# One program block for the first block's stages from retention to routing, with waits in place of the barriers between them

## The chip, the cores and the metric

The kernel runs on one core of a Trainium2 chip. The metric is the device time of one execution in microseconds (us), the median over runs. TensorE (PE in the profile) multiplies matrices and writes into PSUM. VectorE (DVE) and ScalarE (ACT) work on tiles in SBUF and PSUM, GpSimd (POOL) works on SBUF, and SyncE (SP) mostly issues transfers. Each of the five has its own instruction queue, and they are kept in step by semaphores.

## The reference, cut to what matters

The program computes one pass through three different model blocks on 512 tokens of width 1024. The change touches only the first of them:

```python
h = modulate(rms_norm(x, g_mix), sh_a, sc_a)
u = h @ w_in
rq, rk, rv, rg, aq, ak, av, ga, gb = jnp.split(u, pts, axis=-1)
ret = retention(rq, rk, rv, rg)
att = dilated_attention(aq, ak, av, rel_bias)
merged = jax.nn.sigmoid(ga) * (ret @ w_ret_o) + jax.nn.sigmoid(gb) * (att @ w_att_o)
x = x + gt_a[:, None, :] * (merged @ w_o)
h = modulate(rms_norm(x, g_ffn), sh_f, sc_f)
x = x + gt_f[:, None, :] * moe(h, w_router, b_router, w1, b1, w2, b2)   # top 4 of 32 experts
```

`retention` has four heads. `dilated_attention` has four heads in each of three groups. `moe` begins with router scores, the choice of four experts per token and the lists of tokens by expert; after that come the experts' matrices.

## The kernel before

**The stages.** `block1` runs, in this order: the entry with the first modulation sections (`enter`); `retention`; `sigmoid_gate` for the first gate (stage `gate_a`); `linear_split` for the retention's output matrix (`ret_o`); `dilated` (stage `att`, with the later modulation sections between its heads); `sigmoid_gate` for the second gate (`gate_b`); `attention_out` (`att_o`, L2792 on); `add_residual` (`w_o`, with the second norm); `route`; `mixture` (the experts).
**Weights.** They stream through `ring`, six slots of one chunk each. SP issues the transfer of chunk n + 6 when chunk n has been used (`refill`, L171; semaphore `chunk_used`). Most products are full-precision results made of two rounded parts: a chunk has two halves ("places"), ACT rounds a half into `split_w` (L318, the high part), POOL subtracts to get the low part (L323), and PE then does 24 products for the half (high by high, low by high, high by low; L523, L397, L720). Place 0 of `split_w` becomes free when PE has used place 0 of the chunk before (`first_used`), place 1 when it has used the whole chunk before (`chunk_used`). `SplitAhead` lets a stage make place 0 of the next stage's first chunk at its end. `Forward` goes further at the end of retention: both halves of the first chunk of `gate_a` are made and multiplied there, around the transposes of the last head's output (L1454).

**Order of work on an engine.** It is the order in which the functions are written. In a `linear_split` stage ACT rounds the two halves for unit j and then takes the results of unit j - 1 out of PSUM (`take`); only the last unit's result is taken with nothing behind it but the barrier. In `route` ACT first rounds two halves of the experts' first chunk (`act_first_high`, L2213) and then copies the router's partial sums (L2067). DVE does small preparations, then `dve_low` (L2219), then the logits (L2100) and the whole choice. PE begins with eight products of the router's weights with `hT` (L2020). `hT` is written just ahead of it by `Norm.act_evac` (L959, four tiles of it by ACT) and `Norm.dve_evac` (L996, the other four by DVE).

Of the kernel before, what the change touches and what calls it, by code (L numbers as in the profile page):

```python
# [28 lines left out]
KD = D // P  # L29
# [52 lines left out]
class Kit:  # L82

    def __init__(self, nc, ctx, A, out, stream):
        self.nc, self.ctx, self.A, self.out, self.stream, self.scoped = nc, ctx, A, out, stream, []
        self.ring = self.sb(ctx, "ring", [P, RING, SLOT])
# [20 lines left out]
        self.x_source, self.x_loaded = A["x"][0].rearrange("(t p) d -> p t d", p=P), self.sem("x_loaded")  # L108

# [90 lines left out]
def linear(K, stage, kind, src, per_unit, act=None, dve=None, act_runs_ahead=2):  # L200
# [19 lines left out]
    with nc.Block() as block:  # L220
# [323 lines left out]
def linear_split(K, stage, kind, src, per_unit, act=None, dve=None, act_runs_ahead=2, paired=True, tiles=None,  # L544
                 after=None, guests=(), lead=None, parts=None, hold=False, loads=None, onward=None,
                 source=None, aside=None, asked=False):
# [16 lines left out]
    with ExitStack() as ctx:  # L563
# [22 lines left out]
        def split_source(eng, i):  # L586
# [79 lines left out]
        def tensor(pe):  # L666
# [108 lines left out]
        if not hold:  # L775
            with nc.Block() as block:
# [342 lines left out]
def enter(K, C, M, norm, onward):  # L1119
# [6 lines left out]
    with nc.Block() as block:  # L1126
# [180 lines left out]
def enter_turned(K, dst, pair, asked):  # L1307

    with ExitStack() as ctx:  # L1310
        N = Norm(K, "b2_norm", ctx, K.mods3[:, 0, :], None, dst, pair, K.x)
        onward = Onward(K, "b2_qkv", "N", pair, N)
        with K.nc.Block() as block:
# [24 lines left out]
def add_residual(K, stage, src, per_unit, gate=None, norm=None, final=None, guests=(), lead=None, parts=None, loads=None,  # L1338
                 onward=None, source=None, asked=False):
# [7 lines left out]
    def dve(j, banks, wait_tile):  # L1347
        for t in range(NT):
# [9 lines left out]
            if norm and j:  # L1358
# [3 lines left out]
                 guests=guests, lead=lead, parts=parts, loads=loads, onward=onward, source=source, asked=asked)  # L1362
# [47 lines left out]
def retention(K, pair, retpair, spare, name, rel, hot, jobs):  # L1410
# [9 lines left out]
    with ExitStack() as ctx:  # L1420
# [16 lines left out]
        with nc.Block() as block:  # L1437
# [159 lines left out]

def sigmoid_gate(K, stage, pair, dst):

    linear_split(K, stage, "T", pair, 1,
           act=lambda j, banks: K.nc.scalar.activation(dst[:, 2 * j:2 * j + 2, :], banks, ACT.Sigmoid))
# [105 lines left out]
def dilated(K, pair, attT, T0, T12, M):  # L1708
# [11 lines left out]
    with ExitStack() as ctx:  # L1720
# [10 lines left out]
        with nc.Block() as block:  # L1731
# [6 lines left out]
            def _(pe):  # L1738
# [16 lines left out]
                for h in range(AH):  # L1755
# [3 lines left out]
                    for g in range(AG):  # L1759
                        W.tiles(pe, n + g, pair, ps[:, 2 * g:2 * g + 2, :])  # L1760
                        if h and g == 0:
                            M.pe_total(pe, 2 * h - 1)
                    if h:
                        pe.wait_ge(copied, 4 * h)
                        pe.wait_ge(M.evac, 2 * h)
                    W.tiles(pe, n + 3, pair, ps[:, 6:8, :])
# [102 lines left out]
            def _(ve):  # L1869
# [15 lines left out]
                M.dve_spread(ve)  # L1885
                for h in range(AH):
# [18 lines left out]
                M.dve_mods(ve, 1)  # L1905

# [64 lines left out]
def route(K, R, mix):  # L1971
# [4 lines left out]
    A = K.A  # L1976
# [11 lines left out]
    with ExitStack() as ctx:  # L1988
# [18 lines left out]
        with nc.Block() as block:  # L2007
# [9 lines left out]
            def _(pe):  # L2017
                pe.wait_ge(K.loads, K.loads_n)
                for k in range(KD):
# [2688 lines left out]
```

## Time and profile before

| what | us |
|---|---|
| median of 3 runs | 3601.08 |
| lowest and highest run | 3599.22, 3602.8 |
| span of the profiled execution, first to last instruction | 3591.9 |
| what lies around the span, against the median | 9.2 |
| PE busy in the span | 3383.5 |
| DVE, ACT, POOL busy | 2046.8, 1772.5, 1050.0 |
| from the end of `enter` to the start of the experts, about | 690 (94 to 783) |

The page of the profile gives busy time by engine, the span in 40 slices, the queues and the costliest groups. The trace behind it can be asked for a timeline of a stretch (which merges equal instructions of an engine), for busy time and granted clock in given windows, and for what one line waited for.

### The profile page before, as it was taken

How to read it: one execution, taken by the hardware profiler on the slowest of the kernel's cores; microseconds unless marked ns; L12 is line 12 of the kernel's file. 1: busy time of each engine (PE TensorE's matmuls, PEld its weight loads, DVE VectorE, ACT ScalarE, POOL GpSimd, SP SyncE). 2: the span in 40 equal slices, each digit the busy share in tenths (PEclk: the TensorE clock that was granted, in tenths of full speed). 3: DMA queues.
4: the chain of work that ended last, by engine and by line, in shares of the span. 5: the costliest groups of instructions: out<-in, count | busy, mean ns of one | idle time of the engine just before them, and what ended most of it. 6: DMA issues, size and time to landing. Idle time of an engine off the chain costs nothing. (4 is left out here: it accounts for less than half of the span.)

```text
span 3591.9 us, 55463 instructions
## 1 busy us (share of the span) xinstructions
PE 3383.5 (94%) x20916; PEld 2733.5 (76%) x20916; DVE 2046.8 (57%) x2356; ACT 1772.5 (49%) x2340; POOL 1050.0 (29%) x432
## 2 busy tenths in 40 slices
PE   7999999979999999999999898899999987799997
PEld 4877777668888888888888683678887766678876
DVE  3320122179999999999999725411153155346665
ACT  3222333258888878788887624332243343133333
POOL 1324222212323232323232140144443310034443
PEclk9999999989999999999999999999999988899999
DMA  8213343349999999999999637133222310022221
GB/s 282 87 59 100 119 135 121 96 173 391 368 387 369 385 370 384 373 381 375 382 375 380 238 107 282 49 94 94 94 94 71 95 42 4 8 70 94 94 94 41
DMA packets 247189, 696.30 MB, mean 194 GB/s; under 512 B 19806, under 2 KB 151634, under 8 KB 188420
## 3 DMA queue, kind: packets, MB, share of 16 engines
q1 hardware_dynamic: 237140, 658.52, 49.3%
q0 software_dynamic: 9792, 35.66, 3.7%
q8 instruction: 111, 1.82, 0.2%
q14 instruction: 34, 0.28, 0.0%
q10 hardware_dynamic: 112, 0.03, 0.0%
HBM read 668.90 MB, written 29.71 MB: 194 GB/s over the span
## 5 line engine op out<-in xcount | busy, mean ns | idle before, releaser
L323 POOL TENSOR_TENSOR split_w<-ring,split_w 128x1024 fp32r<-128x1024 f32 (+1 forms) x294 | 699.3, 2379 | 1624.1 <-ACT split_w L318 1453.1
L2219 DVE TENSOR_TENSOR moe_low<-ring,moe_high 128x2048 fp32r<-128x2048 f32 x408 | 929.4, 2285 | 57.4 <-ACT moe_high L2209 52.2
L2209 ACT ACTIVATE moe_high<-ring 128x1024 fp32r<-128x1024 f32 x810 | 833.3, 1063 | 122.9 <-PE psum L2460 121.8
L318 ACT ACTIVATE split_w<-ring 128x1024 fp32r<-128x1024 f32 (+1 forms) x294 | 304.3, 1036 | 999.0 <-PE psum L523 597.1
L2456 PE MATMUL psum<-moe_high,moe_xe 128*128 128x512 f32 x2176 | 585.4, 391 | 0.0
L2456 PEld LDWEIGHTS psum<-moe_high,moe_xe 128*128 128x128 f32 x2176 | 410.0, 188 | 82.7
L2368 POOL DMA_INDIRECT moe_y_rows<-moe_ye,moe_target x33 | 193.5, 5864 | 645.1 <-DVE moe_ye L2275 645.1
L523 PE MATMUL psum<-pair,split_w 128*128 128x512 f32 x1488 | 337.9, 389 | 0.0
L2460 PE MATMUL psum<-moe_low,moe_xe 128*128 128x512 f32 x1088 | 336.7, 391 | 0.1
L523 PEld LDWEIGHTS psum<-pair,split_w 128*128 128x128 f32 x1488 | 279.2, 188 | 58.8 <-issue 0.9
L523 PE MATMUL psum<-b_pair,split_w 128*128 128x512 f32 x1344 | 313.3, 395 | 7.0 <-POOL split_w L323 3.9
L523 PEld LDWEIGHTS psum<-b_pair,split_w 128*128 128x128 f32 x1344 | 255.0, 190 | 63.1 <-issue 5.7
L2456 PE MATMUL psum<-moe_high,moe_aT 128*128 128x512 f32 x1088 | 301.9, 399 | 0.0
L2460 PEld LDWEIGHTS psum<-moe_low,moe_xe 128*128 128x128 f32 x1088 | 204.4, 188 | 43.8 <-DVE moe_low L2219 0.5
L523 PE MATMUL psum<-b_hpair,split_w 128*128 128x512 f32 x1008 | 228.6, 389 | 0.0
L2456 PEld LDWEIGHTS psum<-moe_high,moe_aT 128*128 128x128 f32 x1088 | 196.8, 188 | 35.8
L523 PEld LDWEIGHTS psum<-b_hpair,split_w 128*128 128x128 f32 x1008 | 189.2, 188 | 39.3
L2460 PE MATMUL psum<-moe_low,moe_aT 128*128 128x512 f32 x544 | 167.9, 390 | 0.0
L720 PE MATMUL psum<-split_w,b_hpair 128*128 128x512 f32 x672 | 156.8, 395 | 7.3 <-DVE b_hpair L600 7.1
L720 PEld LDWEIGHTS psum<-split_w,b_hpair 128*128 128x128 f32 x672 | 127.9, 191 | 35.9 <-issue 9.2
L720 PE MATMUL psum<-split_w,pair 128*128 128x512 f32 (+1 forms) x720 | 144.1, 361 | 3.3 <-DVE pair L600 1.8
L494 PE MATMUL psum<-split_w,b_pair 128*128 128x256 f32 x1152 | 144.3, 288 | 2.0 <-DVE hT L1665 1.8
(644 smaller groups left out, 4299.3 us busy)
## 6 DMA issues: line engine op xcount, KB each, us to landing
ring<-in_w_experts SPq DMA_DIRECT2D x408, 1024.0 KB, 8.8
ring<-in_w_mod SPq DMA_DIRECT2D x48, 1024.0 KB, 6.0
ring<-in_w_in SPq DMA_DIRECT2D x39, 1024.0 KB, 5.2
ring<-in_w_up SPq DMA_DIRECT2D x33, 1024.0 KB, 5.1
ring<-in_w_in SPq DMA_DIRECT2D x44, 512.0 KB, 5.3
ring<-in_w_down SPq DMA_DIRECT2D x20, 1024.0 KB, 5.0
ring<-in_w_gate SPq DMA_DIRECT2D x11, 1024.0 KB, 5.3
ring<-in_w_out SPq DMA_DIRECT2D x8, 1024.0 KB, 5.5
```

The costliest lines, as they stand in the source:

```text
L318: self.nc.scalar.activation(high, raw, ACT.Copy).then_inc(self.K.rounded, 1)
L323: self.nc.gpsimd.tensor_tensor(low, raw, high.bitcast(F32), ALU.subtract).then_inc(self.K.split, 1)
L494: ins = self.nc.tensor.matmul(out, x(a, r0 + k), w[:, b, k, :], start=(opens and r0 + k + a + b == 0), stop=(closes and r0 + k == KD - 1 a ...
L523: ins = self.nc.tensor.matmul(out[:, tile, :], w[:, a, k, cols], pair[:, b, r0 + k, :], start=(r0 + k + a + b == 0), stop=(r0 + k == nk - ...
L720: ins = nc.tensor.matmul(out[:, t, 0:width], x[:, a, k, t * P:(t + 1) * P], w[:, b, k, :], start=(r + k + a + b == 0), stop=(r + k == tota ...
L2209: self.nc.scalar.activation(self.B["high"][:, j % HALVES, :], self.raw(j), ACT.Copy).then_inc(self.high, 1)
L2219: self.nc.vector.tensor_tensor(flat(self.low_of(j, 2)), self.K.ring[:, self.ring_slot(j // 2), :], high, ALU.subtract).then_inc(self.low, 2)
L2368: self.nc.gpsimd.indirect_dma_start(self.B["y_rows"], bass.IndirectOffsetOnAxis(ap=self.B["target"][:, 0:1], axis=0), self.B["ye"][:, :], ...
L2456: nc.tensor.matmul(out, lhs[:, part, k0 + k, :], high[:, k, :], start=(k0 + k + part == 0 and not started), stop=False)
L2460: ins = nc.tensor.matmul(out, lhs[:, 0, k0 + k, :], low[:, k, :], start=False, stop=(k0 + k == KD - 1))
```

## The change

Two helpers are added to `Kit`: `joined()` opens one block and keeps it, and `stage()` gives out the kept block, or a new one where none is kept. All stages ask `K.stage()`. `block1` opens `joined()` ahead of `retention` and closes it behind `route`, so eight stages share one block and seven barriers go. The barriers ahead of `retention` and behind `route` stay. Where a barrier kept two accesses to the same memory in order, a wait on a semaphore stands now: `vacated` (PE, ahead of writing PSUM banks that the stage before still reads), `room` (ACT, ahead of the first result of `gate_b`), `entry` (SP, ahead of the routing tables' loads), `made` (ACT, ahead of rounding the source of `w_o`), and single waits in `dilated` and `route`. No product, copy or transfer is added, taken away or put in another order.

```diff
+    @contextmanager
+    def joined(self):
+        with self.nc.Block() as self.block:
+            yield
+        self.block = None
+    @contextmanager
+    def stage(self):
+        if self.block is not None:
+            yield self.block
+        else:
+            with self.nc.Block() as block:
+                yield block
...
@@ linear_split
+                if made:
+                    made(eng, r + nr)
                 eng.activation(high, src[:, r:r + nr, :], ACT.Copy).then_inc(a_high, 1)
...
+            if entry:
+                entry(sp)
...
             for j in range(units):
+                if vacated and j < flight:
+                    vacated(pe, j)
...
@@ retention
+    def vacated(pe, j):
+        if j == 1:
+            pe.wait_ge(low_done, RH)
...
@@ sigmoid_gate
+    def act(j, banks):
+        if j == 0 and room:
+            K.nc.scalar.wait_ge(room, 1)
+        return K.nc.scalar.activation(dst[:, 2 * j:2 * j + 2, :], banks, ACT.Sigmoid)
...
@@ dilated
+                        if h == 0:
+                            vacated(pe, g)
...
+                ve.wait_ge(tables.spread, 16 * len(tables.jobs))
...
+    def emptied(pe, j):
+        if j == 0:
+            pe.wait_ge(M.evac, 2 * AH - 1)
+        if j == 3:
+            pe.wait_ge(M.evac, 2 * AH)
+            pe.wait_ge(copied, 4 * AH)
...
@@ route
                 for k in range(KD):
+                    pe.wait_ge(norm.by_dve if k % 2 else norm.by_act, k // 2 + 1)
...
+                sc.wait_ge(norm.turned, KD)
                 X.act_first_high(sc, 0)
...
+                ve.wait_ge(norm.by_act, KD // 2)
                 nc.vector.tensor_copy(B["ps_row"], R.slots[:, 5:6]).then_inc(X.esel, 1)
...
@@ block1
+                joint.enter_context(K.joined())
...
+                    linear_split(K, "ret_o", "T", retpair, 1, vacated=lambda pe, j: pe.wait_ge(K.act_evac, act0 + j + 1),
...
+                        attention_out(K, attT, merge, source, lambda pe, j: pe.wait_ge(K.act_evac, act1 + 2 * j + 2))
...
+                             vacated=lambda pe, j: pe.wait_ge(K.dve_evac, dve1 + j + 1),
+                             entry=lambda sp: sp.wait_ge(K.dve_evac, dve1 + 2),
+                             made=lambda sc, rows: sc.wait_ge(K.dve_evac, dve1 + (rows + 3) // 4))
...
+            joint.close()
             mixture(K, mix)
```

ACT between `retention` and `gate_a`, before: the first row takes the last head's output, the first row behind the barrier rounds place 0 of the second chunk of `gate_a`, the next place 1.

```order
L1512 ACTIVATE b_retpair<-psum 128x1024 [waits ret_transposed]
L1437 UNCONDITIONAL_BRANCH
L780 UNCONDITIONAL_BRANCH [waits barrier_Pool_Activation_PE_DVE_SP_release]
L318 ACTIVATE split_w<-ring 128x1024 [waits first_used,slot3_landed]
L318 ACTIVATE split_w<-ring 128x1024 [waits chunk_used,slot3_landed]
L1602 ACT_TABLE_LOAD
L1602 ACTIVATE b_merged<-psum 128x1024 [waits chunk_used]
```

The same place after:

```order
L1536 ACTIVATE b_retpair<-psum 128x1024 [waits ret_transposed]
L803 UNCONDITIONAL_BRANCH
L335 ACTIVATE split_w<-ring 128x1024 [waits first_used,slot3_landed]
L335 ACTIVATE split_w<-ring 128x1024 [waits chunk_used,slot3_landed]
L1633 ACT_TABLE_LOAD
L1633 ACTIVATE b_merged<-psum 128x1024 [waits chunk_used]
```

The wait for the release is gone with its branch; a branch stays, and the waits that each instruction had of its own.

PE between `w_o` and `route`, before: the last transposes of the norm, then the router's products.

```order
L911 MATMUL psum<-identity,b1_norm2_xn 128x128 [waits b1_norm2_normed]
L911 MATMUL psum<-identity,b1_norm2_xn 128x128 x7
L776 UNCONDITIONAL_BRANCH
L2016 UNCONDITIONAL_BRANCH [waits barrier_Pool_Activation_PE_DVE_SP_release]
L2020 MATMUL psum<-hT,rt_w 32x512 [waits loads]
L2020 MATMUL psum<-hT,rt_w 32x512 x7
L2026 MATMUL psum<-rt_sums,moe_ye 128x32 [waits rt_part_copied,rt_sums]
```

The same place after:

```order
L934 MATMUL psum<-identity,b1_norm2_xn 128x128 [waits b1_norm2_normed]
L934 MATMUL psum<-identity,b1_norm2_xn 128x128 x7
L2063 UNCONDITIONAL_BRANCH
L2068 MATMUL psum<-hT,rt_w 32x512 [waits b1_norm2_by_act,loads]
L2068 MATMUL psum<-hT,rt_w 32x512 [waits b1_norm2_by_dve]
```

Behind the last row here stand three more such pairs and then the same row as before. Each product waits for its own tile of `hT`, in place of one wait for everything.

## Rows read from the trace of the kernel before

**Rows 1.** Page, part 1: busy us, share of the span, instructions.

```profile
PE 3383.5 (94%) x20916; PEld 2733.5 (76%) x20916; DVE 2046.8 (57%) x2356; ACT 1772.5 (49%) x2340; POOL 1050.0 (29%) x432
```

**Rows 2.** Timeline, retention to gate_a: start, us, engine, line, count, [idle before, releaser].

```profile
234.37 5.73 PE L397 MATMUL psum<-b_pair,split_w 128*128 128x512 f32 x24
234.65 1.03 ACT L1512 ACTIVATE b_retpair<-psum 128x1024 fp32r<-128x1024 f32 x1 [4.97 <-PE psum L1454]
235.71 1.22 DVE L1550 TENSOR_TENSOR b_retpair<-psum,b_retpair 128x1024 fp32r<-128x1024 f32 x1 [2.24 <-ACT b_retpair L1512]
...
240.45 2.00 ACT L318 ACTIVATE split_w<-ring 128x1024 fp32r<-128x1024 f32 x2 [4.78 <-PEq L1437]
241.59 4.67 POOL L323 TENSOR_TENSOR split_w<-ring,split_w 128x1024 fp32r<-128x1024 f32 x2 [15.76 <-ACT split_w L318]
...
243.98 2.50 PE L523 MATMUL psum<-b_pair,split_w 128*128 128x512 f32 x5 [3.88 <-POOL split_w L323]
```

**Rows 3.** Timeline, gate_a to ret_o; last row: line 523, ns min/median/max.

```profile
279.34 1.02 ACT L1602 ACTIVATE b_merged<-psum 128x1024 f32<-128x1024 f32 x1 [4.32 <-PE psum L523]
...
280.95 3.42 PE L523 MATMUL psum<-b_retpair,split_w 128*128 128x512 f32 x14 [1.66 <-PEq L776]
...
L523 PE MATMUL psum<-b_retpair,split_w x192: 388/389/467, 281.0 to 324.3; 128*128 128x512 f32 x192
```

**Rows 4.** Timelines, PE's first row of att, gate_b, att_o and w_o.

```profile
326.31 3.91 PE L523 MATMUL psum<-b_pair,split_w 128*128 128x512 f32 x16 [1.58 <-PEq L776]
...
627.83 6.43 PE L523 MATMUL psum<-b_pair,split_w 128*128 128x512 f32 x20 [1.53 <-PEq L1731]
...
674.61 27.70 PE L2817 MATMUL psum<-b_attT,ring 128*128 128x512 f32 x64 [1.37 <-PEq L776]
...
708.28 5.72 PE L707 MATMUL psum<-split_w,b_pair 128*128 128x512 f32 x24 [0.47 <-PEq L2792]
```

**Rows 5.** Windows, PE: stretch, us, PE busy (instructions), granted clock, DMA share, GB/s.

```profile
242.30:249.10 6.80, 5.12 (x12) 0.50 0.35 122
244.00:249.00 5.00, 5.00 (x12) 0.50 0.11 36
250.00:255.00 5.00, 5.00 (x24) 1.00 0.00 0
624.60:628.00 3.40, 1.26 (x3) 1.00 0.91 348
628.00:631.40 3.40, 3.40 (x9) 0.50 0.69 257
```

**Rows 6.** Timeline, w_o to route.

```profile
754.69 2.78 ACT L959 ACTIVATE hT<-psum,b_mods 128x512 f32<-128x512 f32 x4 [4.18 <-PE psum L911]
754.80 2.96 DVE L996 TENSOR_SCALAR hT<-psum,b_mods 128x512 f32<-128x512 f32 x4 [3.30 <-PE psum L911]
...
758.07 2.00 ACT L2213 ACTIVATE moe_high<-ring 128x1024 fp32r<-128x1024 f32 x2 [0.59 <-PEq L776]
758.08 3.40 PE L2020 MATMUL psum<-hT,rt_w 128*32 128x512 f32 x16 [2.67 <-PEq L776]
...
760.18 2.29 DVE L2219 TENSOR_TENSOR moe_low<-ring,moe_high 128x2048 fp32r<-128x2048 f32 x1 [0.82 <-ACT moe_high L2213]
...
761.55 0.60 ACT L2067 ACTIVATE moe_ye<-psum 128x512 f32<-128x512 f32 x1 [1.48 <-PE psum L2020]
...
763.38 0.29 DVE L2100 TENSOR_TENSOR rt_lg<-psum,rt_b 128x128 f32<-128x128 f32 x1 [0.91 <-PE psum L2026]
```

**Rows 7.** The queues' own rows at the barriers: ns min/median/max, when.

```profile
L1437 PEldq DRAIN  x1: 4288/4288/4288, 235.9 to 235.9; - x1
...
L1437 ACTq EVENT_SEMAPHORE  x1: 17/17/17, 240.3 to 240.3; - x1
```

**Rows 8.** Page, part 3: instruction fetches: packets, MB, share of 16 engines' span.

```profile
q8 instruction: 111, 1.82, 0.2%
```

**Rows 9.** Windows of all engines, the third model block's quiet stretch (busy us, clock).

```profile
2900.00:3240.00 340.00, 277.22 (x6054) 225.41 (x6055) 164.83 (x274) 113.76 (x212) 34.79 (x14) 0.88 0.08 24
```

More of the change, by code:

```diff
@@ L219, in linear @@
     ahead = SplitAhead(K, last)
-    with nc.Block() as block:
+    with K.stage() as block:
         @block.sync
@@ L545, in linear_split @@
                  after=None, guests=(), lead=None, parts=None, hold=False, loads=None, onward=None,
-                 source=None, aside=None, asked=False):
+                 source=None, aside=None, asked=False, vacated=None, entry=None, made=None):
     nc = K.nc
@@ L775, in linear_split @@
         if not hold:
-            with nc.Block() as block:
+            with K.stage() as block:
                 block.sync(sync)
@@ L1125, in enter @@
     ahead = SplitAhead(K, last)
-    with nc.Block() as block:
+    with K.stage() as block:
         @block.sync
@@ L1312, in enter_turned @@
         onward = Onward(K, "b2_qkv", "N", pair, N)
-        with K.nc.Block() as block:
+        with K.stage() as block:
             @block.sync
@@ L1361, in add_residual @@
     linear_split(K, stage, "N", src, per_unit, dve=dve, paired=False, tiles=tiles, after=after,
[L1362 removed]
+                 guests=guests, lead=lead, parts=parts, loads=loads, onward=onward, source=source, asked=asked,
+                 vacated=vacated, entry=entry, made=made)
 RH, RDK, RDV = 4, 128, 256
@@ L1436, in retention @@
         ps = K.ps
-        with nc.Block() as block:
+        with K.stage() as block:
             @block.sync
@@ L1730, in dilated @@
         l = K.sb(ctx, "att_sum", [P, 2])
-        with nc.Block() as block:
+        with K.stage() as block:
             @block.sync
@@ L2006, in route @@
         spread = K.sb(ctx, "rt_spread", [P, 2, SPILLS])
-        with nc.Block() as block:
+        with K.stage() as block:
             @block.sync
@@ L2632, in mixture @@
         B["low1"] = K.sb(ctx, "moe_low1", [P, HALVES - 2, HALF], F32R)
-        with nc.Block() as block:
+        with K.stage() as block:
             @block.sync
@@ L2791, in attention_out @@
     ahead, evac0 = SplitAhead(K, last), K.dve_evac_n
-    with nc.Block() as block:
+    with K.stage() as block:
         @block.scalar
@@ L2877, in group_norm @@
         spread = ms[:, :].unsqueeze(2).to_broadcast([P, groups, width])
-        with nc.Block() as block:
+        with K.stage() as block:
             @block.vector
@@ L2902, in turn_tiles @@
     turned, copied = K.sem(f"{name}_turned"), K.sem(f"{name}_copied")
-    with nc.Block() as block:
+    with K.stage() as block:
         @block.tensor
@@ L2940, in diff_attention @@
         section = lambda u: u - BEGIN if 0 <= u - BEGIN < 12 else None
-        with nc.Block() as block:
+        with K.stage() as block:
             @block.sync
@@ L3097, in rest_projections @@
         turn_bank = (1, 2, 3, 4, 5, 6, 7, 0)
-        with nc.Block() as block:
+        with K.stage() as block:
             @block.sync
@@ L3220, in mixture_tail @@
         by_head = lambda rows: rows.rearrange("p (g d) -> p g d", d=GDV)
-        with nc.Block() as block:
+        with K.stage() as block:
             @block.tensor
@@ L3807, in prepare @@
         w2, a2, selT = K.sb(ctx, "rp_w2", [P, 512]), K.sb(ctx, "rp_a2", [P, 512]), K.sb(ctx, "rp_selT", [P, P])
-        with nc.Block() as block:
+        with K.stage() as block:
             @block.sync
@@ L3853, in causal_attention @@
         av_out = lambda u: ps[:, 6, (u % 2) * P:(u % 2 + 1) * P]
-        with nc.Block() as block:
+        with K.stage() as block:
             @block.sync
@@ L3985, in shifted_features @@
     with nc.sbuf_tensor("rw_prev", [P, 2, 2, S + 1], F32) as prev:
-        with nc.Block() as block:
+        with K.stage() as block:
             @block.vector
@@ L4045, in rwkv_scan @@
         y_last = lambda m: y[:, 2:4, :].rearrange("p t (c m d) -> p t m c d", m=2, d=HD)[:, :, m, :, :]
-        with nc.Block() as block:
+        with K.stage() as block:
             @block.sync
@@ L4335, in rwkv_finish @@
         spread = lambda a, h: a[:, h, :].unsqueeze(2).to_broadcast([P, groups, HD])
-        with nc.Block() as block:
+        with K.stage() as block:
             @block.sync
```

42 lines of the change are left out of this document (25 added, 17 removed).

## The prediction

> **What bounds the kernel now.** I read the page first. TensorE (PE) is busy for 94% of the span, so no other engine bounds the program as a whole [rows 1]; but in this share sit gaps, and the change aims at those. The waits of the stretch from 240 to 783 us tell which gaps they are: at each of the seven places where one stage ends and the next begins PE sat idle, and the releaser of the idle time is a queue at the barrier, or (once) what the barrier held back [rows 2 to 4, 6]. I then took the timeline at each of the seven, and the windows, for the granted clock. The reader is to see three things. Between retention and gate_a PE idles for 3.88 us, because ACT could begin to round the next half only after the barrier, and POOL's low part comes behind it [rows 2]. At the other five entries ahead of route PE idles for 0.47 to 1.66 us, and its next operands were already there [rows 3, 4]. At route all engines wait, but what ends last behind the wait is ACT and DVE, not PE [rows 6]. Work on the path is conserved: nothing behind route runs against a fixed instant, since the ring is refilled when chunks are used. So what PE, or the chain in route, gains moves everything behind it.
>
> **What a removed gap is worth.** The record of a product is longer than its turn: its median is 0.39 us [rows 3], and 24 products take 5.73 us, so one turn is (5.73 - 0.39) / 23 = 0.23 us [rows 2]. When the next product follows in its turn, 0.39 - 0.23 = 0.16 us more than the recorded idle is won. I add 0.16 to each of the six entries where PE goes on with products.
>
> **Retention to gate_a: 3.88 + 0.16 = 4.04 us.** ACT's last work in retention ends at 234.65 + 1.03 = 235.68 [rows 2]. The half that it must round next (place 0) waits for first_used, which the first 24 products of Forward gave ahead of the transposes, before 234.37. So now ACT rounds it from 235.7 (1.0 us), POOL subtracts until about 236.8 + 2.4 = 239.2, and PE, whose current 24 products end at 240.1, finds it ready. Place 1 waits for chunk_used at 240.1: ACT until 241.2, POOL until 243.7, while PE is busy with place 0 until 240.1 + 5.5 = 245.6. The cover is 1.9 us. The added wait (low_done, given at 235.71 + 1.22 = 236.93) is met 3 us early.
>
> **Gate_a to ret_o: 1.66 + 0.16 = 1.82 us.** Here one order bites. ACT takes the last unit out of PSUM (1.02 us from 279.34) ahead of rounding place 1 for the next stage, which in the middle of a stage it does the other way round [rows 3]. Rounding takes 2.00 / 2 and the low part 4.67 / 2 us [rows 2]. So PE, from 279.3 on place 0, needs place 1 at 279.3 + 5.5 = 284.8, and gets it at 279.34 + 1.02 + 1.0 + 2.4 + 0.2 for semaphores = 284.0. The cover is 0.8 us. It holds, and if it did not, the price would be the lack alone. The added waits (act_evac) ask for units taken 10 us and more ago, the last excepted, and that one is asked for 30 us later.
>
> **The next four entries.** Ret_o to att: 1.58 + 0.16 = 1.74. Att to gate_b: 1.53 + 0.16 = 1.69. Gate_b to att_o: 1.37 + 0.16 = 1.53. Att_o to w_o: 0.47 + 0.16 = 0.63 [rows 4]. In all of them place 0 was made ahead, and the results that the added waits ask for were read out well before, except DVE's last merge in att_o, which ends while PE is on the 24 products that it does ahead for w_o, and is asked for behind them. Queued behind SP's new wait (entry) are the routing tables' loads and the ring refills of w_o: the barrier held them until just before 708.28, the wait only until that merge ends, so nobody gets them later. Behind ACT's waits (made, room) stands ACT's own work in that stage; both are met when it arrives.
>
> **W_o to route: 1.5 us.** PE stood idle for 2.67 us, but PE is not what ends last. Without the barrier ACT ends the tiles of hT at 757.47 and rounds its two halves at once, until 757.5 + 2.0 = 759.5, in place of 760.07; then dve_low runs from 759.6 to 761.9, and the logits on DVE begin at 761.9 in place of 763.38: 1.5 us [rows 6]. PE's branch is shorter: the last of its eight products can begin at 757.76 + 0.05 when DVE has written the last tile, and takes under 1.7 us even at half the clock (its pairs took 3.40 / 4 = 0.85 each, two deep), so ACT copies from about 759.5, 2 us sooner, and the logits reach DVE by 761.6. The bounds are 0.6 (all that ACT gains, 0.59) and 2.7 (all that PE gains). I take 1.5, which is DVE's. Behind it the chain is the old one, up to GpSimd's gather and the barrier that stays.
>
> **The clock: 4.2 us.** Between 242.3 and 249.1 the granted clock was 0.50, that is 1.2 GHz in place of 2.4, and it fell while PE stood still at the barrier and behind it. PE worked in it for 5.12 us at half rate: 12 records touch five us there, 24 a few us later at clock 1.00 [rows 5]. Half of 5.12 is lost, 2.5 us. The same at gate_b: PE was busy for 1.26 of 3.40 us ahead of it, and then worked from 627.83 to 631.4 at 0.50, which loses half of 3.6, say 1.7. With the gaps closed PE is busy throughout at the first place, and at the second for about 1.26 + 1.7 of the 3.4 us; the loops over heads have such stretches at clock 1.00. I take both back: 4.2; the other bound is 0. The Trainium skill has the rule behind it (TensorE: Matmul & The Clock Gate, Part 1: The HAM clock gate): the throttled state is the default and activity releases it, so an idle engine pays again when it restarts. By that, the trace agrees at both places, and a change that only shortened the gaps would be worth less than one that closes them.
>
> **The sum.** 4.04 + 1.82 + 1.74 + 1.69 + 1.53 + 0.63 = 11.45 for the six entries, 1.5 for route, 4.2 for the clock: 17.1 us. Against the profiled execution that is 3591.9 - 17.1 = 3574.8 of span; with the 9.2 us around it, 3584.0. A measurement of this kernel tells about 0.2%, 7.2 us, from no change: a time under 3593.9 would be faster.
>
> **Rival 1: the waits go, the clock does not come back** (or falls at other instants instead). For it: when the clock falls depends on what PE did shortly before, and the shift changes which idle stretches count. Then 12.95 us are won: 3588.1.
>
> **Rival 2: the branches cost what the barrier hid.** Each engine still jumps from stage to stage. A fetch of instructions takes 0.2% of 16 x 3591.9 us over 111 packets, about 1.0 us each [rows 8]. Were one exposed at each of the seven entries, 7.3 us would be given back: 3591.3. Against it: PE's queue had been worked off up to the barrier 4.29 us before it emptied [rows 7], so PE has that much cover, and behind the release at 240.3 ACT began at 240.45, branch included [rows 2, 7]. The Trainium skill speaks for it (Advanced Engine Details and Errata, ISA Cache: few cache lines of 256 instructions); no row shows a branch that missed.
>
> **Rival 3: it does not do what it says.** If what PE waited for at the entries were not the barrier but something hidden under it, a new wait would take the place of each. For this speaks only the first entry, where the releaser is POOL. Then the chip shows 3595 to 3601.
>
> **Rival 4, slower: the clock falls more often behind the change.** Place: the third model block, where small operations leave PE waiting and the mean clock over 340 us is 0.88, so that it runs at half rate for 0.24 x 340 = 82 us [rows 9]. The shift moves these stretches against the instants at which the clock is set. Each us more at half rate costs up to 0.5 us, so it decides from 34 us more, a mean clock under 0.83 there, and from about 50 us more it makes the kernel 0.2% slower, 3608. Against it: the three runs lie within 3.6 us, and they too meet these instants at chance.
>
> **How the numbers follow.** Forecast 0.66, rival 1 0.15, rival 2 0.08, rival 3 0.08, rival 4 0.03. The first three are all faster by over 0.2%: 0.89; rival 3 is the same: 0.08; slower 0.03. The range reaches from 3579 (route at its upper bound of 2.7, a run as lucky as the lowest, and a stretch at half clock less) to 3592, which takes in rivals 1 and 2.
>
> **What the profile of the changed kernel would show.** PE: no idle time with a barrier's queue as releaser between 240 and 750 us, and a gap of under 0.3 us at the six entries. Clock 1.00 from 235 to 255 and through the start of gate_b. POOL's first row of gate_a at about 236.8 by the old clock of the timeline, ahead of PE's end of Forward. At gate_a to ret_o place 1 is ready 0.8 us before PE asks; a gap on PE some 5.5 us into ret_o, released by POOL, would show this step wrong. In route the logits begin 4.4 us after the last hT tile of ACT, in place of 5.9. The experts begin about 17 us sooner than 783. The prediction fails if PE has gaps of 1 us or more at the entries still, with new releasers, or if the stretch up to the experts is 17 us shorter and the rest is longer.

## The result, and the profile after

The changed kernel takes 3573.08 us (median of 5 runs, 3568.77 to 3583.65) beside 3599.22 for the kernel before on the same chip (5 runs, 3596.05 to 3602.80). The ratio is 0.9937, interval 0.9927 to 0.9948: faster, by 26 us where 17 were forecast and the range ended at a gain of 22. Three sets of runs of the changed kernel give 3573.08, 3577.34 and 3574.62. Over the 73 runs of before made ahead of the shifted kernel and the 11 of after in the last two sets, the means are 3598.15 and 3575.15, 23.0 us apart, with a standard error of about 1.2. This is the size to be explained.

The page after, part 1, answers [rows 1]:

```profile
PE 3393.0 (95%) x20916; PEld 2742.7 (77%) x20916; DVE 2047.6 (57%) x2356; ACT 1772.6 (49%) x2340; POOL 1037.1 (29%) x432
```

The work is the same: 20916 products, 2356 and 2340 instructions of DVE and ACT. The span is 3581.8 and the same execution was timed at 3583.65, so only 1.8 us lie around a span.

The timeline of after, retention to gate_a, answers [rows 2] (start, us, engine, line, count, [idle before, releaser]):

```profile
234.30 5.73 PE L414 MATMUL psum<-b_pair,split_w 128*128 128x512 f32 x24
234.58 1.03 ACT L1536 ACTIVATE b_retpair<-psum 128x1024 fp32r<-128x1024 f32 x1 [4.97 <-PE psum L1478]
235.51 1.05 ACT L335 ACTIVATE split_w<-ring 128x1024 fp32r<-128x1024 f32 x1
236.64 2.39 POOL L340 TENSOR_TENSOR split_w<-ring,split_w 128x1024 fp32r<-128x1024 f32 x1 [10.87 <-ACT split_w L335]
239.87 10.36 PE L540 MATMUL psum<-b_pair,split_w 128*128 128x512 f32 x45
```

ACT rounds right behind the copy that it ends retention with. POOL has the low part at 239.03, before PE is through with its 24 products, and PE goes on without idle time, where it idled 3.88 us.

PE's rows at the five entries that follow, from its timelines, answer [rows 3, 4]; one that stands without a bracket had no idle time ahead of it:

```profile
272.51 1.75 PE L540 MATMUL psum<-b_retpair,split_w 128*128 128x512 f32 x7
...
316.03 1.29 PE L540 MATMUL psum<-b_pair,split_w 128*128 128x512 f32 x5
...
614.86 1.10 PE L1098 MATMUL psum<-mod_later_parts,mod_later_heads 128*128 128x512 f32 x2 [1.00 <-ACT mod_later_parts L1105]
615.39 16.93 PE L540 MATMUL psum<-b_pair,split_w 128*128 128x512 f32 x72
...
659.35 3.16 PE L2877 MATMUL psum<-b_attT,ring 128*128 128x512 f32 x7
...
692.27 1.98 PE L730 MATMUL psum<-split_w,b_pair 128*128 128x512 f32 x8
```

None of the six entries has a gap, and no barrier's queue appears as releaser. Windows of all engines (us, then busy time with instructions of PE, PEld, DVE, ACT, POOL, granted clock, DMA share, GB/s) of the same 636 us, before and then after:

```profile
94.00:730.00 636.00, 613.89 (x3068) 496.79 (x3067) 135.43 (x228) 184.65 (x236) 197.56 (x86) 0.99 0.33 103
```

```profile
94.00:730.00 636.00, 624.37 (x3139) 507.66 (x3138) 147.19 (x239) 192.33 (x248) 202.39 (x88) 1.00 0.33 104
```

The clock no longer falls in this stretch: 1.00 throughout, and 71 products more have been done by 730.

The timeline of after, w_o to route, answers [rows 6]:

```profile
734.35 4.94 PE L934 MATMUL psum<-identity,b_norm_xn 128*128 128x128 f32 x28 [1.09 <-ACT b_norm_xn L892]
738.56 2.79 ACT L982 ACTIVATE hT<-psum,b_mods 128x512 f32<-128x512 f32 x4 [4.18 <-PE psum L934]
739.49 3.25 PE L2068 MATMUL psum<-hT,rt_w 128*32 128x512 f32 x16 [0.20 <-ACT hT L982]
741.23 2.01 ACT L2263 ACTIVATE moe_high<-ring 128x1024 fp32r<-128x1024 f32 x2
743.34 2.29 DVE L2269 TENSOR_TENSOR moe_low<-ring,moe_high 128x2048 fp32r<-128x2048 f32 x1 [0.53 <-ACT moe_high L2263]
745.55 0.28 DVE L2150 TENSOR_TENSOR rt_lg<-psum,rt_b 128x128 f32<-128x128 f32 x1
```

PE begins the router's products 0.93 us behind the start of ACT's first tile of hT, in place of 3.39. The logits begin 4.20 us behind ACT's last tile (738.56 + 2.79 = 741.35), in place of 5.91. DVE's low part ends last ahead of them, as forecast.

**A ledger up to the experts.** The next table is worked out from the traces: the time from one PE product to another, the same two in every kernel. "Before" and "after" are three traces each. The starts are those of the first product at the places named.

| stretch | before | after | gain | forecast |
|---|---|---|---|---|
| end of retention to gate_a | 9.30 | 5.25 | 4.05 | 4.04 |
| gate_a to ret_o | 36.97, 36.98, 37.25 | 32.64 | 4.33 | 1.82 + 2.5 clock |
| ret_o to att | 45.35 to 45.39 | 43.52 | 1.83 | 1.74 |
| att to gate_b | 301.53 to 301.57 | 299.36 | 2.2 | 1.69 |
| gate_b to att_o | 46.74 to 46.78 | 43.97 | 2.8 | 1.53 + 1.7 clock |
| att_o to w_o | 33.67 | 32.92 | 0.75 | 0.63 |
| w_o to the experts' first products | 75.00, 75.06, 75.09 | 72.21, 72.82, 72.17 | 2.7 | 1.5 |
| start to the experts in full work (at 800 us in before) | 788.22, 788.28, 788.81 | 769.16, 769.74, 770.25 | 18.7 | 17.1 |
| from there to the end | 2775.88, 2782.18, 2782.05 | 2785.27, 2775.93, 2776.36 | 0.8 | 0 |

So the traces show 18.7 us up to the experts, and behind them a scatter from one execution to the next of 6 us in before and 9 in after. The experiments ask whether the ledger is right in its parts, and where the 4 us are that the mean of the runs has and the ledger has not.

### The profile page after: what moved, and what is told of

The parts are those of the page before. It is cut to its first block and busy times, and to the rows that moved or that the text cites. A ratio compares the mean times of both kernels' runs of the same rounds, so it can differ in the third digit from the quotient of the medians.

```text
span 3581.8 us, 55403 instructions
## 1 busy us (share of the span) xinstructions
PE 3393.0 (95%) x20916; PEld 2742.7 (77%) x20916; DVE 2047.6 (57%) x2356; ACT 1772.6 (49%) x2340; POOL 1037.1 (29%) x432
## 3 DMA queue, kind: packets, MB, share of 16 engines
q8 instruction: 111, 1.82, 0.2%
## 5 line engine op out<-in xcount | busy, mean ns | idle before, releaser
L511 PEld LDWEIGHTS psum<-split_w,b_pair 128*128 128x128 f32 x1152 | 143.4, 197 | 5.4 <-DVE hT L1699 2.8
```

The costliest lines, as they stand in the source:

```text
L511: ins = self.nc.tensor.matmul(out, x(a, r0 + k), w[:, b, k, :], start=(opens and r0 + k + a + b == 0), stop=(closes and r0 + k == KD - 1 a ...
```

## Experiments

### The first barrier alone, all but the first, all but the last

```diff
@@ block1, changed kernel, behind gate_a: the first barrier alone is removed
+                    joint.close()
@@ block1, changed kernel, from ahead of retention to behind it: all but the first
-                joint.enter_context(K.joined())
...
+                    joint.enter_context(K.joined())
@@ block1, changed kernel, route ahead of which the joint block ends: all but the last
-            route(K, tables, mix, norm)
             joint.close()
+            route(K, tables, mix, norm)
```

> Only the barrier between retention and gate_a is removed; the shared block is closed behind gate_a, the other barriers stand. Theory: PE's first product of gate_a starts 4.05 us earlier than before, the clock stays at 1.00 there, and ret_o starts 6.5 us earlier (280.95 becomes 274.4). Nothing more is won up to gate_b's entry (gate_b's first product at 621.2 +- 0.6). Rival (the clock falls there anyway, or the gain needs the neighbours' barriers gone too): ret_o starts only 4 us earlier.

> All barriers of the change removed but the one between retention and gate_a. Theory: gate_a's first product at 244 +- 0.4 and a half-clock stretch behind it as before; the experts' first transposes at 783.3 - 19.0 + 6.5 = 770.8 +- 0.7. Rival (gains add up differently, because one gap hides another): more than 1.5 us off that.

> The changed kernel with the barrier between w_o and route kept (the shared block is closed ahead of route). Theory: up to the last transposes of the norm all as in the changed kernel (16.4 us ahead of before); the logits chain then starts with the old gaps, so that the placing products (768-770 us before) are only 16.4 ahead and the experts' first transposes 16.4 +- 0.5, against 18.1 and 19.0 in the changed kernel. Open is the last 0.9 us between those two: if it is also due to this barrier it goes here, if it is due to where the stage lies against something else it stays.

PE's rows at the entry concerned, each from the timeline of its kernel:

```profile
240.10 10.14 PE L540 MATMUL psum<-b_pair,split_w 128*128 128x512 f32 x44
...
274.52 1.85 PE L540 MATMUL psum<-b_retpair,split_w 128*128 128x512 f32 x7 [1.62 <-PEq L114]
```

```profile
244.26 6.26 PE L540 MATMUL psum<-b_pair,split_w 128*128 128x512 f32 x14 [3.98 <-POOL split_w L340]
```

```profile
741.50 3.25 PE L2068 MATMUL psum<-hT,rt_w 128*32 128x512 f32 x16 [2.51 <-PEq L114]
```

Removing the first barrier alone shortens retention to gate_a to 5.25 us, brings 2.55 us of clock in the next stretch, and leaves every later entry as it was (45.51, 301.65, 46.84). Its single run took 3589.92 us. Keeping only the first one leaves 9.38 there and wins all the rest (single run 3584.11). Keeping only route's wins every entry and nothing in route: 34.47 us from the norm's transposes to the experts' first products, where before has 34.55 and after 31.88 (single run 3585.11). Two things cancel in this 34.47: 28 of the transposes happened to run longer at half clock (5.93 us in place of 4.94), and the 0.9 us that the expectation left open were won although the barrier stood. So the price of each barrier does not hang on the others, and the sum over entries is allowed. One miss: with the first barrier kept, the experts began at 771.87 us and not at 770.8, of which 0.4 stand in gate_a (35.57, where 36.97 - 1.82 = 35.15 was due).

### The clock without touching a barrier

```diff
@@ linear_split, PE, kernel before (first filler kernel)
+            if stage == "gate_a":
+                for _ in range(14):
+                    nc.tensor.matmul(K.ps[:, 7, :], src[:, 0, 0, 0:P], src[:, 0, 0, :], start=True, stop=True)
@@ dilated, PE (second filler kernel, besides the first)
                     turn_output(4 * h + 3)
+                for _ in range(3):
+                    nc.tensor.matmul(ps[:, 0, :], pair[:, 0, 0, 0:P], pair[:, 0, 0, :], start=True, stop=True)
                 M.pe_total(pe, 2 * AH - 1)
+                for _ in range(4):
+                    nc.tensor.matmul(ps[:, 0, :], pair[:, 0, 0, 0:P], pair[:, 0, 0, :], start=True, stop=True)
```

> The kernel before, all barriers kept, with 14 extra products of TensorE (3.2 us at full clock) whose results nobody reads, behind the barrier at the start of gate_a, where it stood idle for 3.9 us waiting for POOL. Theory (the clock fell because PE stood still): the first product that counts still starts at 244.0, the clock is 1.00 behind it or its half stretch is shorter by half at least, and ret_o starts 1.2 to 2.5 us earlier than 281.0. Rival (the clock falls for another reason, or the fillers delay the real products): ret_o within 0.3 of 281.0 or later.

> The kernel before with all its barriers, and with unread products that only fill idle time of PE: 14 at the start of gate_a (as in the first filler kernel), 3 ahead of the last modulation sum of att and 4 behind it, ahead of the barrier to gate_b. Asked: how much of the gain over all runs is the clock. Theory A (block 1 loses 2.5 us at gate_a and 1.7 us at gate_b at half clock, and no more): the stretch up to the experts is 3.5 to 4.5 us shorter than before, less up to 0.5 us for what the fillers delay, and the median of the timed runs is 3593 to 3596 beside a before of about 3597.5. Rival B (the barriers set off more half clock in most executions than the few traces show, and that is the part of the gain that the traces up to the experts lack): the median is 3590 to 3592. Rival C (what the filler saves at gate_b is lost elsewhere, as in the trace of the first filler kernel, where 6.8 us at half clock stood at gate_b): 3595 to 3598.

The timeline of PE in the first, and a window of all engines in the second:

```profile
239.29 3.42 PE L673 MATMUL psum<-b_pair 128*128 128x512 f32 x14 [0.32 <-PEq L1440]
```

```profile
616.00:634.00 18.00, 16.36 (x84) 11.51 (x83) 2.43 (x8) 4.89 (x7) 7.13 (x3) 1.00 0.33 118
```

The barrier stands, its release comes as late as ever, and products that nobody reads fill the wait for POOL. Gate_a to ret_o falls from 36.97 to 34.59: 2.4 us, the forecast 2.5. With the second set the clock is 1.00 through gate_b's start, and gate_b to att_o falls from 46.76 to 45.17: 1.6, the forecast 1.7. So what the clock term said of these two places is shown. But the timed runs of the second kernel give 3596.82 (12 runs) beside 3598.73, ratio 0.9995, interval 0.9985 to 1.0004: about 2 us of the 4 arrive, with an error as large. The median lies in the range of rival C and not in that of theory A, though the trace of this kernel shows the saving at both places; where the other 2 us went was not found. In the first filler kernel gate_b lost more than before (47.98, with 6.8 us at half clock from 623.6), so the same gap does not always cost the same.

### More barriers

```diff
@@ block1, kernel before, between ret_o and att
+                    for _ in range(4):
+                        with K.nc.Block() as block:
+                            @block.sync
+                            def _(sp):
+                                sp.nop()
```

> The kernel before with four empty program blocks added between ret_o and att, so five barriers in a row stand where one did. Theory (a barrier costs mostly because PE drains and restarts its pipeline and the last results are waited for, once): each further one costs 0.2 to 0.7 us, att starts 1 to 3 us later than 326.3. Rival (each barrier has its full price of 1.8 us by itself): att starts 7 us later.

PE's timeline, and two windows as above:

```profile
328.01 6.16 PE L523 MATMUL psum<-b_pair,split_w 128*128 128x512 f32 x20 [3.26 <-PEq L2753]
```

```profile
324.00:327.30 3.30, 0.75 (x4) 0.29 (x2) 1.23 (x1) 0.00 (x0) 0.00 (x0) 1.00 0.45 122
327.30:330.70 3.40, 2.69 (x6) 2.15 (x7) 1.12 (x6) 1.06 (x1) 1.51 (x1) 0.53 0.77 312
```

Four barriers with nothing between them add 3.26 - 1.58 = 1.7 us of idle time, 0.43 each. The longer gap then brings 3.4 us at 1.2 GHz where ret_o to att had none before: att to gate_b takes 302.91 in place of 301.53. So a bare barrier costs 0.43. The ones between working engines cost 0.75 to 2.2 in the ledger, clock apart, and part of that is the wait for the last results: at gate_a to ret_o PE stops at 279.29, and ACT's copy of the last result ends at 279.34 + 1.02 = 280.36, so 1.07 of the 1.66 us are that copy [rows 3]. A gap that is long enough costs clock as well. The single timed run, 3594.57, lies below the mean of before in spite of the added barriers; it says nothing beside a scatter of 15 us.

### The rest: both kernels again

> The kernel before once more, unchanged, timed against itself. Theory A (the change wins 19 us up to the start of the experts, and what it seemed to win or lose behind them is scatter of the half-clock stretches): ratio 1.000 within 0.002, times within about 8 us of each other, and the time from the experts' first transposes (783.3 us in the first trace) to the end differs from the 2808.6 us of the first trace by up to 8 us, in step with the mean granted clock. Theory B (the stretch behind the experts' start gains by the change): this stretch is within 2 us of 2808.6 here.

> The changed kernel once more, unchanged. Theory A: the experts' first transposes start at 764.3 us again (within 0.7), 19 us before those of the kernel before; the whole is 17 to 25 us faster, and over this and the first comparison the mean gain goes to 19 or 20. Theory B: the whole is again 24 to 28 us faster, with the same 19 us at the experts' start.

> The kernel before, unchanged, for a further trace and five further rounds. If the traces so far are typical, the stretch from the start to the experts' first products is 788 +- 0.7 us and the rest 2772 to 2785. If they were lucky ones, this trace shows 790 or more up to there, with half-clock stretches in block 1 that the first two lack. Over all runs the mean should stand 22 to 23 us above the mean of the changed kernel; a difference of 19 to 20 here would say that the mean so far was drawn high by scatter.

> The changed kernel, unchanged, for a further trace and five further rounds. Expected up to the experts' first products 769 to 770 us and no half clock between 94 and 730 us, rest 2772 to 2785. Median 3574 to 3579; ratio to before 0.9935 to 0.9947 if the gain is about 20 to 22.7 us.

The unchanged kernels gave 3596.89 and 3598.52 (12 runs each), and 3577.34 and 3574.62 (5 and 6 runs; ratios 0.9941, interval 0.9928 to 0.9953, and 0.9931, interval 0.9918 to 0.9943). The traces agree up to the experts, as the table has it, so the first traces were no lucky ones there. The difference of 22 to 23 us over all runs held.

### The same work, later

```diff
@@ retention, PE, changed kernel (shifted)
                     n = first + 3 * h
+                    if h == 2:
+                        for _ in range(82):
+                            nc.tensor.matmul(ps[:, 0, :], pair[:, 0, 0, 0:P], pair[:, 0, 0, :], start=True, stop=True)
@@ build, both kernels (late)
+            with nc.Block() as late:
+                @late.vector
+                def _(ve):
+                    for _ in range(16):
+                        K.dve_link(nc.vector.memset(K.hT[:, 0:2, :], 0.0))
             K.scope(block1)
```

> The changed kernel with 82 unread products on PE in the middle of retention (82 turns of 0.2275 us = 18.7 us of pure work at full clock): all that follows runs 18.7 us later, so the experts begin when they begin in the kernel before, but block 1 has no inner barriers. Asked: the timed runs say that the change is worth 23 us (mean 3598.15 over 73 runs of before, 3575.15 over 11 of after), the traces up to the experts 18.7; where are the 4 left? Theory A: chance in the part behind the experts' start, or a gain that does not hang on when that part runs: the mean here is 3575.2 + 18.7 = 3593.9, and before stays 4 above it. Theory B: the part behind loses more or less to the clock depending on when it runs, so with the same start as in before it takes as long as in before: mean 3596.8 to 3598.2. In the trace of both: start to experts 788.4 +- 0.7, no half clock between 230 and 750 us.

> The changed kernel with a program block of its own ahead of everything, in which DVE alone fills a tile 16 times (some 17 us): the whole program runs later by that much, with no product of TensorE added. The delay D is read from the trace (start of the first product, 8 us in the kernels without it). Theory P (position: how long the part behind the experts' start takes hangs on when it runs, counted from the program's start): mean = 3575.15 + D + about 8, as in the kernel shifted by products. Theory F (the unread products cost later: they raised that kernel's remaining part, not its position) or theory C (chance): mean = 3575.15 + D, +- 1.5.

> The kernel before with the same delay D at its start. Theory F or C: mean = 3598.15 + D, +- 1. Theory P: a deviation from that of several us, of either sign, while the kernels behind the delay are the same. Difference to the delayed changed kernel: 23 by F, anything from 15 to 27 by P.

| kernel | later by, trace | mean of the runs | expected from addition | off by |
|---|---|---|---|---|
| after, 82 products in retention | 18.0 | 3600.61 (11 runs, error 0.8) | 3593.2 | +7.4 |
| after, DVE alone ahead of all | 19.9 | 3595.63 (12 runs, error 1.1) | 3595.1 | +0.5 |
| before, DVE alone ahead of all | 19.1 | 3611.22 (6 runs, error 1.3) | 3617.25 | -6.0 |

The delay is read at the end of retention, against the mean of the three traces of the same kernel without it. The unread products of the first kernel in PE's timeline:

```profile
149.78 6.74 PE L1494 MATMUL psum<-b_pair 128*128 128x512 f32 x29
```

With the error of the mean that each is compared with, the last column is uncertain by 1.3 to 1.6. It is much larger than that in two cases out of three, and it has both signs. The first kernel fits neither of its theories: its mean lies above the 3593.9 of A and above the 3596.8 to 3598.2 of B. The delayed changed kernel is as theories F and C had it, the delayed kernel before as P had it. In the kernel before, the same delay changes what the clock does: windows of all engines at gate_a and at gate_b of that trace, 19.1 us later than in [rows 5]:

```profile
256.00:272.00 16.00, 12.11 (x48) 9.56 (x48) 0.24 (x1) 5.37 (x5) 5.12 (x3) 0.89 0.19 66
636.00:652.00 16.00, 12.74 (x75) 8.92 (x74) 2.47 (x8) 4.17 (x8) 4.76 (x2) 1.00 0.38 131
```

The gap at gate_b is there, and the clock stays at 1.00; gate_b to att_o takes 45.14, as with the fillers, and gate_a to ret_o 35.72. Each barrier still costs what it cost (9.29, 45.37, 33.67). So the price of a barrier at full clock is fixed, and what the clock adds behind it is not: it changed with when the gap came. The Trainium skill says so in its own way (TensorE: Matmul & The Clock Gate, Part 1: The HAM clock gate): the same kernel shows a different number of slow products from run to run, depending on the gate's phase when it starts. That agrees with 46.8, 48.0 and 45.1 for one stretch of unchanged code. The Trainium skill, in the same section, puts the penalty of the ramp at under 1% of a typical span and advises against fitting the number of slow products. Here 1% would be 36 us, more than the whole change, so for this comparison the advice is no help.

What this does not settle: whether the 7.4 us of the first row come from the position too, or from the unread products. Only part of them can be the clock: its runs have 186.5 us at half clock (worked out as below) where after has 179.3, and 7.2 us more at half clock can cost 3.6 at most. The second row stands some 4 us further at the experts' start, and is not off. Position counted from the program's start alone explains neither pair.

### A version with the clock kept up in route

```diff
@@ add_residual, PE, changed kernel, ahead of the norm's transposes
+            if stage == "w_o":
+                pe.wait_ge(after.x_ready, NT)
+                for _ in range(7):
+                    nc.tensor.matmul(K.ps[:, 3, :], source.own[:, 0, 0, 0:P], source.own[:, 0, 0, :], start=True, stop=True)
@@ route, PE, ahead of the placing; one product each stands at its end and behind the experts' first transposes
+                for _ in range(2):
+                    nc.tensor.matmul(K.ps[:, 0, :], K.hT[:, 0, 0:P], K.hT[:, 0, :], start=True, stop=True)
```

> The changed kernel plus extra products of TensorE that nobody reads, in its idle times around route: seven ahead of the norm's transposes, four short ones (two full-width fp32 products) ahead of the placing products, one each at the end of route and behind the experts' first transposes. Theory (half clock follows idle PE): the 20.5 us half-clock stretch around the experts' start shortens or goes, the first experts' products run at full rate from 768.9 on, and the loop is 1.5 to 3 us further ahead than in the changed kernel. Rival (too little work to keep the clock, and fillers at half clock delay the chain): 0 to 2 us later than the changed kernel.

```profile
730.59 1.75 PE L755 MATMUL psum<-b_pair 128*128 128x512 f32 x7
...
734.59 3.28 PE L938 MATMUL psum<-identity,b_norm_xn 128*128 128x128 f32 x28 [1.09 <-ACT b_norm_xn L896]
```

The 28 transposes take 3.28 us in place of 4.94, and norm to the router's sums 9.61 in place of 10.96 to 11.83; the other fillers won nothing (30.52 us from the norm's transposes to the experts, and 30.40 in the shifted kernel, which has none of them). The trace is 1.1 to 1.3 us ahead at the experts' first products, and 0.8 to 2.2 with the experts in full work. The runs give 3575.54 (5 runs), ratio 0.9947, interval 0.9933 to 0.9961: no different from the changed kernel. The shifted kernel had 9.61 there with no filler at that place, by chance alone.

## Why the prediction was wrong in size

**Where the 10.9 us went.** The forecast was 3584.0, the median 3573.08. Of the difference 2.9 us are the base (3601.08 for a mean of 3598.15), 2.1 are the draw of the first five runs (the mean of after is 3575.15), and 5.9 are the gain, 23.0 for 17.1. Of these 5.9, the six entries have about 0.65 and route 1.2, the clock at its two places gave 0.4 less than forecast, and 23.0 - 18.7 = 4.3 (error 1.2) stand, by subtraction, behind the experts' start, where the sum had no term. So three steps failed: the chain behind the logits was taken for the old one, the clock's part was read from two stretches of one trace and set at nothing elsewhere, and the base with its range came from three runs.

**Splitting the gain by the clock.** Every run lists its span and mean clock c, so its time at half clock is 2 x (1 - c) x span. On average that is 195.5 us in before (error 1.3) and 179.3 in after (error 2.3), 16.2 fewer. If half of every such microsecond were lost, that would be worth 8.1 us, and 14.9 would be left at full speed. But 8.1 is an upper bound, since PE also stands idle in that time: in the 16 traces it is busy for 73 to 81% of the half-clock time behind the experts' start, and over the 73 runs of before each microsecond more at half clock goes with 0.24 us more (0.31 over the 16 of after). By those prices the clock's part is 4 to 5 us. The prediction had 12.95 (11.45 and 1.5) without the clock and 4.2 by it.

**The six entries: right.** The ledger gives 4.05 + 1.8 + 1.83 + 2.2 + 1.5 + 0.75 = 12.1 for 11.45, where the two stretches with clock are taken less 2.5 and 1.3. In the second, product by product, before loses 1.27 us more in gate_b's first 5.4 us, and 1.53 at the entry to att_o. The one term mis-sized among them is gate_b's. I added 0.16 us to each recorded gap for the overlap of a record with the next turn, a figure from products with 0.39 us of record. Ahead of gate_b stand two products of the modulation whose record is 1.10 us long while the next product starts 0.53 us behind it. There the hidden part is 1.10 - 0.53 = 0.57, and 1.53 + 0.57 = 2.1 is what came.

**Route: mis-sized, 2.7 in place of 1.5.** The step itself holds: from the norm's transposes to the logits 12.91 us became 745.55 - 734.35 = 11.20, so 1.7, and DVE is what sets it. The step that failed is "behind it the chain is the old one, up to GpSimd's gather". Timelines of before and then after, from DVE's cast to the gather:

```profile
771.50 0.17 DVE L2129 CAST rt_gcol<-moe_gsplit 128x8 fp32r<-128x8 f32 x1
...
777.55 1.12 POOL L2345 DMA_INDIRECT moe_xg<-moe_h_rows,moe_source  x1 [38.16 <-SPq L2007]
```

```profile
753.66 0.17 DVE L2179 CAST rt_gcol<-moe_gsplit 128x8 fp32r<-128x8 f32 x1
...
758.80 1.12 POOL L2395 DMA_INDIRECT moe_xg<-moe_h_rows,moe_source  x1 [35.53 <-DMA moe_h_rows<-rt_tokens]
```

The gather waits until the tokens' rows are stored: 6.05 us behind the cast before, 5.14 after. (The bracket of before names SP's queue, whose branch at 776.7 follows the same store.) In the three traces of before, those of both filler kernels, of more barriers and of the first barrier alone it is 5.96 to 6.05, and the queue view of these microseconds has one row more, which after lacks:

```profile
q14 instruction: 1, 0.01, 0.2%
```

It is absent in the three traces of after, in the kernels with all but one barrier removed and in the shifted one, all at 5.13 to 5.15, and in the version with the clock kept up (5.36). The changed kernel with the delay ahead has it, and 5.95. The kernel before with that delay has 5.15, and its fetch ran between 785 and 786 us, 2 us ahead of the cast (787.73) and of the stores behind it. So in all 16 traces the 0.6 to 0.9 us go with a fetch of instructions that falls among the stores, and not with the barriers: the kernel that keeps route's has the gain, and the changed kernel delayed has lost it. What makes the fetch fall there was not tried.

**The clock: right at its two places, set at nothing elsewhere.** 2.5 and 1.7 were forecast at gate_a and gate_b. The traces and the two filler kernels show 2.4 and 1.3 to 1.6. What failed is that I took the two stretches of one trace for the whole of the clock's part. The 4.3 us that the ledger lacks lie behind the experts' start, in code that the change does not touch. The clock can hold 1.7 to 3.6 of them: of the 16.2 us fewer at half clock, 9.1 lie ahead of the experts in full work (49.9 us in the traces of before, 40.8 on average in those of after), and the other 7.1 are worth 0.24 to 0.5 each. The rest, 0.7 to 2.6 us, is hardly more than the error, and its cause stays open. With all started 19 to 20 us later the two kernels are 3611.22 - 3595.63 = 15.6 us apart (error 1.7) in place of 23.0, or 16.4 with the delays made equal. So some 15 us (14 without the fetch) are won clear of the clock, as the ledger has it, and what comes on top was 8 us at one position and 1 at the other. That the forecast of 17.1 lies between the two is no merit of its clock term.

**The base and the range: wrong.** The 9.2 us "around the span" do not exist; there are 1.8. I set the span of one execution, a fast one (3591.9 + 1.8 = 3593.7), against the median of three others, and read chance as a fixed term. It did no harm to the forecast, since it cancels. It did to the range, where three runs within 3.6 us stood for the scatter of a kernel whose 73 runs reach from 3589.65 to 3604.53. Base and gain erred on one side: 3598.15 - 17.1 would have been 3581, still 6 above the mean of after.

**The rivals.** Rival 1 falls: the clock is 1.00 from 94 to 730. Rival 2 falls: with all branches left, no entry has a gap. Rival 3 falls. Rival 4 did not come: after has less time at half clock, not more. Whether its mechanism, the third block's stretches shifted against the clock, gave part of the gain is not shown. Between 2900 and 3240 the three traces of before have 80, 97 and 92 us at half clock; those of after, 19 us earlier and so over about the same work, have 89, 79 and 85: too few to show a cause. I had counted it as a risk alone, though nothing in its argument excluded a gain. **The profile's forecasts** held: POOL at 236.64 (236.8), the logits 4.20 us behind hT (4.4), no gap some 5.5 us into ret_o, the experts 18.8 us sooner (17).

## What to carry to other kernels

Price a barrier between stages by the idle time of the engine that sets the pace, plus what its last record hides (read from the two rows around it, not from a usual product), and look at what the other engines could already do behind it; those sums held to 0.1 us. Keep the clock apart: a stretch at 1.2 GHz behind a gap in one trace is one draw, and a shift of later work draws again, here by up to 6 or 7 us and with either sign. Price time at half clock below one half where PE also waits: here 0.24 to 0.31 us for each. Make the base and the range from spans and clocks of many executions; and where a step says that the chain behind is the old one, list the transfers in it and what may fall among them.

## What the runs showed of the hardware

An empty program block costs 0.43 us when nothing is under way. Fourteen unread products in a wait keep the granted clock at 1.00 and give back 2.4 us right there, yet over their runs the kernels with fillers showed little of it (ratio 0.9995 where 4 us were saved; 0.9947 beside 0.9931 to 0.9941). A program delayed by 19 to 20 us took 0.5 us more than its delay or 6.0 less, according to the kernel, and one delayed by 82 unread products 7.4 more. Over 73 runs of one kernel a microsecond more at half clock goes with 0.24 us more of time. And one fetch of 8 KB of instructions among stores goes with 0.6 to 0.9 us on the path, in 16 of 16 traces; ahead of them it costs nothing there.
